# Recurrence of an RWKV layer: products spread over four quadrants of the TensorE array by exchanging partition halves

## The reference, cut to what matters

```python
def wkv7_scan(r, decay, k, v, kk, a):
    def step(S, inp):
        r_t, w_t, k_t, v_t, kk_t, a_t = inp
        s_kk = jnp.einsum('bhij,bhj->bhi', S, kk_t)
        S = (S * w_t[:, :, None, :] - s_kk[..., None] * (a_t * kk_t)[:, :, None, :]
             + v_t[..., None] * k_t[:, :, None, :])
        return S, jnp.einsum('bhij,bhj->bhi', S, r_t)
    ...
y = wkv7_scan(rh, heads(decay), kh, vh, kk, heads(a))
y = layer_norm(y, LNX_EPS).reshape(B, T, RWKV_WIDTH) * lnx_g + lnx_b
```

## Time and profile before

| what | value |
|---|---|
| median of three runs | 3341.51 us |
| profiled execution, its span | 3339.61 us, 3337.8 us |
| PE busy in the span | 3075.4 us (92%) |
| DVE, ACT, POOL busy | 1552.5, 1104.6, 984.9 us |
| PE instructions | 21074 matmuls |
| the recurrence, first to last product but the turned y | 387.8 to 642.6 us |

### The profile page before, as it was taken

The page is one execution under the profiler, slowest core; times in us unless marked ns, Lnnn a source line. Parts: engine busy times, 40 slices in busy tenths (PEclk is TensorE's granted clock), DMA queues, the critical chain, the costliest instruction groups (busy, mean ns, idle before and its releaser), DMA issues. The chain is left out here.

```text
span 3337.8 us, 50028 instructions
## 1 busy us (share of the span) xinstructions
PE 3075.4 (92%) x21074; PEld 2436.7 (73%) x21074; DVE 1552.5 (47%) x2316; ACT 1104.6 (33%) x1885; POOL 984.9 (30%) x638
## 2 busy tenths in 40 slices
PE   5999799795999998998999999789989999996898
PEld 3886489674888887887877777567778777775676
DVE  3999745434332333244034433378431434424875
ACT  3012333233222222123134434455222444445532
POOL 2442022202333333332233333142223333331421
PEclk8999899897999999999999999899999999998999
DMA  5112400032111111122212112576431122127754
GB/s 205 45 51 85 150 4 4 27 114 95 50 45 49 50 45 40 51 98 89 70 46 82 64 62 84 186 221 186 148 105 52 50 71 82 51 76 261 203 160 140
DMA packets 341929, 308.57 MB, mean 92 GB/s; under 512 B 11328, under 2 KB 300480, under 8 KB 337248
## 3 DMA queue, kind: packets, MB, share of 16 engines
q1 hardware_dynamic: 266944, 242.63, 23.0%
q10 hardware_dynamic: 74784, 63.05, 5.7%
HBM read 248.89 MB, written 54.66 MB: 91 GB/s over the span
## 5 line engine op out<-in xcount | busy, mean ns | idle before, releaser
L1871 PE MATMUL PS<-x_high_sb,w_high_sb 128*128 128x512 f32 x1312 | 530.0, 404 | 0.0
L1871 PE MATMUL PS<-x_high_sb,w_low_sb 128*128 128x512 f32 x1312 | 518.2, 395 | 0.0
L1871 PE MATMUL PS<-x_low_sb,w_high_sb 128*128 128x512 f32 x1312 | 517.4, 394 | 0.0
L1871 PEld LDWEIGHTS PS<-x_high_sb,w_high_sb 128*128 128x128 f32 x1312 | 247.0, 188 | 76.0 <-issue 23.9
L1871 PEld LDWEIGHTS PS<-x_high_sb,w_low_sb 128*128 128x128 f32 x1312 | 246.9, 188 | 57.7
L360 PE MATMUL PS<-h_high_sb,up_high_sb 128*128 128x512 f32 x704 | 274.8, 390 | 13.5 <-POOL up_low_sb L1436 13.5
L1871 PEld LDWEIGHTS PS<-x_low_sb,w_high_sb 128*128 128x128 f32 x1312 | 247.3, 189 | 52.3
L1486 DVE SCALAR_TENSOR_TENSOR z_sb<-PS,cols_sb,z_sb 128x1023 f32<-128x1023 f32 x88 | 112.8, 1282 | 348.5 <-ACT z_sb L1467 342.1
L360 PE MATMUL PS<-h_low_sb,up_high_sb 128*128 128x512 f32 x704 | 274.6, 390 | 0.0
L360 PE MATMUL PS<-h_high_sb,up_low_sb 128*128 128x512 f32 x704 | 274.4, 390 | 0.0
L2109 DVE CUSTOM_DVE_ANT_0 scores_sb<-PS,alibi_sb,sinks_sb 128x256 f32<-128x256 f32 (+1 forms) x256 | 104.4, 464 | 342.2 <-PE PS L1889 342.2
(11 more groups left out here) (405 smaller groups left out, 6090.0 us busy)
## 6 DMA issues: line engine op xcount, KB each, us to landing
w_raw_sb<-w_in SPq DMA_DIRECT2D x102, 512.0 KB, 3.7
up_raw_sb<-w_up SPq DMA_DIRECT2D x44, 512.0 KB, 3.7
ada_slots_sb<-ada_w SPq DMA_DIRECT2D x16, 1024.0 KB, 6.7
attn_raw_sb<-attn ACTq DMA_DIRECT2D x32, 512.0 KB, 5.9
decays_sb<-running_sums SPq DMA_DIRECT2D x16, 1024.0 KB, 7.4
attn_raw_sb<-state_out ACTq DMA_DIRECT2D x32, 512.0 KB, 4.0
xbc<-staged_sb ACTq DMA_DIRECT2D x24, 512.0 KB, 2.6
xbc_sb<-xbc SPq DMA_DIRECT2D x16, 768.0 KB, 9.0
```

The source lines that it names most:

```text
L1871: last = pe.matmul(PS[:, bank, :], a[:, n % 2, k], b[:, k, cols], start=k == 0 and a is WH and b is HH, stop=k == KT - 1 and a is WL)
```

## The change

Nine of a unit's steps (AP1, SQ2a, SQ2b, GV, AP2, SQ3, FR, FF, Z) are given all four quadrants. `by_quarter` takes, for each of its three operands, a rule of where a pair (head parity, chunk) lies. In *plain* all lie by chunk, as before. In *first* the odd heads' chunks have changed partition halves; in *home* chunk c is on half c, but the slots are sorted by which half the chunk came from; in *away* the halves are changed with those slots. Each product reads one layout and writes another, and its result lies in two banks (the number in the table goes from 1 to 2), 256 columns in each. `N` writes the odd heads exchanged, `PB` writes its second half for odd heads exchanged (two products in place of one), and at the copy of the fourth token tile ACT writes four half-partition pieces in place of two whole ones.

`AP1` and `AP2` no longer add to the inverse. DVE writes, beside each power, power plus identity into the (then free) transition tile, and the product with that is simply copied. The products of y with the state leave `S0` and are issued together in `S1`. The table's costs are new, and with them the order.

```diff
-        steps = [("PB", 2, "dve", 1.2), ("N", 2, "dve", 0.6), ("TRa", 2, "act", 1.8), ("SQ1a", 1, "dve", 1.0),
+        steps = [("PB", 2, "dve", 1.1), ("N", 2, "dve", 0.6), ("TRa", 2, "act", 1.8), ("SQ1a", 1, "dve", 1.0),
...
+        quarters = [(f, par, c) for f in range(CT) for par in range(2) for c in range(2)]
+        plain = lambda f, par, c: (half(c), CT * par + f)
+        first = lambda f, par, c: (half(c ^ par), CT * par + f)
+        home = lambda f, par, c: (half(c), CT * (c ^ par) + f)
+        away = lambda f, par, c: (half(c ^ par), CT * c + f)
...
+            def by_quarter(bank, left, left_at, right, right_at, out_at, width=CH, stop=True, check=False):
+
+                for f, par, c in quarters:
+                    (rows, i), (_, j), (out, n) = left_at(f, par, c), right_at(f, par, c), out_at(f, par, c)
+                    at = n % CT * width
+                    last = pe.matmul(PS[out, bank + n // CT, at:at + width], left[rows, i], right[rows, j],
+                                     start=width == CH or f == 0, stop=stop, skip_group_check=check)
+                return last
...
+                        if par == 0:
+                            pe.matmul(PS[half(c), b0, f * P:(f + 1) * P].rearrange("p (a n) -> p a n", a=2), left, right,
+                                      start=True, stop=True)
+                        else:
+                            pe.matmul(PS[half(c), b0 + 1, f * P:f * P + CH], left, right[:, 0], start=True, stop=True)
+                            last = pe.matmul(PS[half(1 - c), b0 + 1, f * P + CH:(f + 1) * P], left, right[:, 1],
+                                             start=True, stop=True)
...
-                    last = by_chunk(b0, PW2[:, g, 0], IB[:, g])
+                    last = by_quarter(b0, PI[:, g], first, IB[:, g], first, home)
...
-                    last = by_chunk(b0, PW2[:, g, 1], PW2[:, g, 0])
+                    last = by_quarter(b0, PW2[:, g, 1], first, PW2[:, g, 0], first, home)
...
-                    last = by_chunk(b0, IB[:, g], XR[:, g], P, True, False, True)
+                    last = by_quarter(b0, IB[:, g], away, XR[:, g], away, home, P, False, True)
...
-                    for f in range(CT):
-                        last = pe.matmul(PS[half(c), 4 * g + 2, hcol(2 * f + c)], RKQ[feat(c), f, chunk(c)],
-                                         state(k, c)[feat(c), f], start=False, stop=True, skip_group_check=True)
+                    for f, d in [(f, d) for f in range(CT) for d in range(2)] if c else []:
+                        last = pe.matmul(PS[half(d), 4 * g + 2, hcol(2 * f + d)], RKQ[feat(d), f, chunk(d)],
+                                         state(k, d)[feat(d), f], start=False, stop=True, skip_group_check=True)
...
-                    for par in range(2):
-                        nc.scalar.copy(XR[:, g, 4 * par:4 * par + 4, 0:HD], tok[:, g, 3].rearrange(
+                    for par, c in [(par, c) for par in range(2) for c in range(2)]:
+                        nc.scalar.copy(XR[half(c ^ par), g, CT * c:CT * (c + 1), 0:HD], tok[half(c), g, 3].rearrange(
                             "p (f a c) -> p a f c", f=CT, a=2)[:, par])
...
-                elif name in ("SQ1a", "SQ2a"):
-                    ins = v.tensor_copy(flat((PW2 if name == "SQ1a" else PW4)[:, g, 0]), B)
-                elif name in ("AP1", "AP2", "AP3"):
+                elif name == "SQ1a":
+                    v.tensor_copy(flat(PW2[:, g, 0]), B)
+                    ins = v.tensor_tensor(PI[:, g], by_head(B), ident_rows, ALU.add)
+                elif name == "SQ2a":
+                    v.tensor_copy(slots(PW4[:, g, 0]), two)
+                    ins = v.tensor_tensor(slots(PI[:, g]), two, ident_of, ALU.add)
+                elif name in ("AP1", "AP2"):
+                    ins = v.tensor_copy(slots(IB[:, g]), two)
+                elif name == "AP3":
                     ins = v.tensor_tensor(flat(IB[:, g]), flat(IB[:, g]), B, ALU.add)
```

More of the change, by code:

```diff
@@ L893, in rwkv_recurrence @@
             for i, (name, n, eng, cost) in enumerate(steps):
[L894 to L898, removed]
+                if name == "GT":
+                    own = (3,)
+                elif n in choice:
+                    own = min((o for o in choice[n] if name != "F2" or not set(o) & set(banks_of["Z"])),
+                              key=lambda o: max(used[b] for b in o))
                 else:
@@ L909, in rwkv_recurrence @@
         count, filled, emptied, before, last_in, done = {"act": 0, "dve": 0}, {}, {}, {}, {}, 0
-        for k, g, name, eng, banks in plan:
+        for k, g, name, eng, own in plan:
             key = (k, g, name)
@@ L918, in rwkv_recurrence @@
             joins = name in ("H1", "H2", "S0", "S1", "YX", "Y")
-            before[key] = [] if joins else sorted({last_in[b] for b in banks if b in last_in})
+            before[key] = [] if joins else sorted({last_in[b] for b in own if b in last_in})
             if eng is not None:
-                for b in banks:
+                for b in own:
                     last_in[b] = key
@@ L957, in _ @@
                     empty(pe, other)
-                b0 = banks[0]
+                b0 = own[0]
                 cols = unit_cols(k)
@@ L1002, in _ @@
                     empty(pe, (k, g, "TRa"))
-                    for f, par, i, h in every:
-                        for c in range(2):
-                            last = pe.matmul(PS[half(c), b0, i * CH:(i + 1) * CH], GR[half(c), g, i, 1],
-                                             v[half(c), hcol(h)], start=True, stop=True)
+                    for f, par, c in quarters:
+                        (rows, i), (out, n) = plain(f, par, c), away(f, par, c)
+                        at = n % CT * CH
+                        last = pe.matmul(PS[out, b0 + n // CT, at:at + CH], GR[rows, g, i, 1], v[rows, hcol(2 * f + par)],
+                                         start=True, stop=True)
                 elif name == "AP2":
@@ L1054, in _ @@
                                       v[half(c), hcol(h)], start=f == 0, stop=False, skip_group_check=True)
[L1055 to L1058 removed]
+                    for f, par, c in quarters:
+                        rows, i = home(f, par, c)
+                        pe.matmul(PS[feat(par), b0 + c, f * HD:(f + 1) * HD], nb[rows, hcol(2 * f + par)],
+                                  WU[rows, g, i, HD:P], start=False, stop=False, skip_group_check=True)
                     for f, par, i, h in every:
@@ L1062, in _ @@
                                       start=h == 0, stop=False, skip_group_check=True)
-                    for f, par, i, h in every:
-                        for c in range(2):
-                            last = pe.matmul(PS[half(c), b0 + 2, hcol(h)], BR[half(c), g, i, 0], WU[half(c), g, i, HD:P],
-                                             start=False, stop=False, skip_group_check=True)
+                    for f, par, c in quarters:
+                        (rows, i), (_, j) = home(f, par, c), plain(f, par, c)
+                        last = pe.matmul(PS[rows, b0 + 2, hcol(2 * f + par)], BR[rows, g, j, 0], WU[rows, g, i, HD:P],
+                                         start=False, stop=False, skip_group_check=True)
                 elif name in ("S0", "S1"):
@@ L1157, in _ @@
             root(TT - 1)
-            for k, g, name, eng, banks in plan[-2:]:
-                turned((k, g, name), banks[0])
+            for k, g, name, eng, own in plan[-2:]:
+                turned((k, g, name), own[0])
         @block.gpsimd
@@ L1253, in _ @@
                 elif name == "MT":
[L1254 to L1255 removed]
+                    ins = v.tensor_tensor(MT[:, g], two, ident_of, ALU.add)
                 elif name == "ZT":
```

96 lines of the change are left out of this document (49 added, 47 removed), and 10 rows, old and new, of the table steps.

## The result

| kernel | median us (runs) | range us | profiled execution us | its span us |
|---|---|---|---|---|
| before | 3341.42 (15) | 3334.11 to 3342.55 | 3339.61 | 3337.8 |
| after | 3346.39 (15) | 3342.53 to 3354.36 | 3345.06 | 3343.3 |

The ratio is 1.0021, 95% interval 1.0013 to 1.0029: the change costs 5 us by the medians, 4 to 10 us by the interval. The forecast was 3343.0 us, "the same".

What follows compares the result with a forecast made beforehand. It took PE's queue as the bound. Full periods +5.0, unit 0 +1.3, two periods without norm work -1.7 and the end -3.1 gave +1.5 us on 3341.5: 3343.0 us, own range 3337 to 3350.

Steps and rivals of the forecast that it cites:

- All six waits: PE waiting for DVE or ACT emptyings before H2, SA, SQ2b, PG, SQ3 and FR: 6.25 us a period.
- PE's step: Each changed 64-wide step on PE takes 0.48 us over four quadrants, bounds 0.44 and 0.60, in place of 0.93.
- rivals on four quadrants: Four quadrants don't overlap in the exchanged order, the eight steps stay at 0.93 us: 3367 us, chance 0.03.
- work that arrives in full or in part: PE's saved work shows up in the time: 3304 us in full, chance 0.05; 3332 in part, chance 0.12.
- The rival of later emptyings: Emptyings come later than walked, mainly from AP1 to SQ3: 1.6 us a period more, 3354 us, chance 0.20.
- the walk: Step-by-step comparison along the new order of PE's own work with the emptying engine's queued work, one period: 31.75 us.
- H2: PE waits before H2 for H1's emptying on DVE, with only TRa between: 1.7 us in place of 0.4.
- FR: PE waits before FR for GV's emptying on ACT, four pieces and the main copy: 1.1 us.
- -3.1 us at the end: FF and Z lie inside the last period and one S0 is short by 0.46 us: -3.1 us together.
- a full period: One recurrence period: 30.7 - 0.4 - 4.8 + 6.25 = 31.75 us, 1.0 us longer, five times.
- The rival did not occur: The clock falls in the recurrence because waits make PE idle: some 50 us, 3390 us, chance 0.03.
- The rule weighed in the prediction: Tiling speeds TensorE but not PSUM emptying, so time comes near the forecast sum; busy shares would give near 3304 us.

Runs made afterwards that it cites:

- Run 3: The changed kernel with all layouts plain, so each changed step uses two quadrants again, same order and additions: 3370.67 us, ratio 1.0091.
- run 6: The changed kernel with the fourth token tile's copy (GV's operand) in two whole pieces, its exchange left out: 3342.97 us, ratio 1.0012.
- Run 4: The changed kernel with y_gated moved on DVE from behind F2 to behind H1: 3338.97 us, ratio 0.9998.
- run 2: The kernel before with the changed table's nominal costs, so only the order changes: 3363.69 us, ratio 1.0068.
- run 7: The changed kernel with a cost table chosen so that the walked order has few waits: 3323.79 us, ratio 0.9951.
- run 12: The changed kernel with a third cost table, from a walk that also limits how fast 253 PE instructions pass: 3323.11 us, ratio 0.9957.
- Run 1: The changed kernel with the planner's old costs, bank counts and all else of the change kept: 3325.27 us, ratio 0.9958.
- run 10: Run 1's kernel measured again, unchanged: 3325.86 us, ratio 0.9956.
- run 8: Run 7's kernel with two more 128x512 products a unit on PE, their result overwritten: 3335.09 us, ratio 0.9990.

## Why the prediction came out as it did

The mechanism was right. All six waits are there, behind the engines named, and in the full periods there is nothing else of size. Two of its signs were missed all the same: the period of F2 goes up to 33.2 us, where 31.2 to 32.2 was said, and PE's busy time in the recurrence is 212.5 us, where about 205 was said. Point by point:

- **PE's step.** Predicted 0.48 us, measured 0.41 to 0.52. Run 3 shows that the quadrants work in the exchanged order. The rivals on four quadrants (3367) and on work that arrives in full or in part (3304, 3332) are out. The rival of later emptyings (3354) holds in part: of its 1.6 us a period 0.55 are there.
- **The emptyings on the path.** Predicted 6.25 us a period. Measured 5.8 us of idle time, to which six tails of about 0.17 us belong, since the walk counts from start to start (0.93 us for a step whose record is 1.10): 6.8 us. With the tails H2 is 1.77 against 1.7, SA 1.19 against 1.2, SQ2b 0.52 against 0.4, PG 1.26 against 1.35, SQ3 0.58 against 0.5, FR 1.50 against 1.1. FR is the largest miss: four pieces took 1.65 us and not 1.24, at the upper end of the bounds given. The walk also named ACT alone for it; by run 6 AP3's emptying on DVE holds FR 0.9 us even where the pieces are short.
- **H2 was right by luck.** DVE took 569.42 - 562.44 = 6.98 us from Y's first instruction to the end of H1's emptying, where the walk had 6.7: y_gated took 0.4 us more by GpSimd's addition beside it. The walk's own numbers give 6.7 - 4.9 = 1.8 us, and 2.0 with the release that the other five places have, where it wrote 1.7. PE also took some 0.4 us more up to H2 (PB with F2, and a pause of 0.21). Without the first H2 would wait 1.4 us. Run 4, which moves y_gated out of both, gives back 7.4 us.
- **The sum.** It had -3.1 us at the end (measured: 21.28 us from the last but one Y to the last product before, 17.96 after, -3.3), and for the six periods from Y to Y -0.85 + 5 x 1.0 = +4.2 us, where 184.51 went to 192.85, +8.3 us. Up to the first Y it had 1.3 - 0.85 = +0.4, and it was +0.2. That agreement is in part luck: the stage starts at the lower clock, which lasted 4.8 us of it before and 2.8 us now, and the walk had no term for it. So the miss, 5.2 against 1.5, is the term "a full period": +1.8 us (32.5 against 30.8 us), and not +1.0. Of the missing 0.8 us, 0.55 are the six waits; that the rest are steps at 0.52 us and pauses fits the rows, but no run separates it.
- **The clock.** The rival did not occur in the profiled execution: behind the first 2.8 us of the stage it stayed at 1.00, with PE idle for 6 of 32 us in pieces of 0.4 to 1.8 us. That was nearer than it looks. In runs 2 and 3 the clock fell once each behind a 1.8 us wait before H2, the very wait that after has (up to 1.81 us), while the same wait in their other periods was followed by no fall. Runs 7 and 12 have seven waits of 2.0 to 2.5 us, and at or behind the end of five of them it fell. Each fall cost 1.7 us; the rival's 50 us had the clock low for a third of the stage. The page "TensorE: Matmul & The Clock Gate" of the Trainium skill warns, under "A second HAM failure mode: psum-queue depth-cycling", of short idle times between groups of products. After's trace doesn't show it; in four other traces single waits of 1.8 to 2.5 us were followed by a fall.
- **The rule weighed in the prediction** held for this order. "TensorEngine Tiling (Array Packing)" of the Trainium skill says, under "Performance Considerations", that the emptying of PSUM may become the bottleneck once tiling makes the products quick; by the engines' busy shares the time would have been 3304 us. Run 1, with the same quick products and 21 us less, shows that it was the order that put the emptyings on the path, not their amount.

Where the prediction was off in kind is what it left unasked: whether the order had to be this one. The same change with the old costs is 21 us faster than with the new ones and 15 to 16 us faster than the kernel before (runs 1 and 10). Of the new orders none was told from it.

What stays open: what a faster order would give if the small operation of Y's emptying didn't meet GpSimd's multiplication. By the rows, run 7 lost 8.2 us to the waits behind it and 3.4 to falls of the clock, run 12 up to 7.3 and 5.1. Taken away in full that would put them near 3312 and 3311 us, an estimate from these rows that no run tests; moving that one multiplication on GpSimd is the run that is missing. Why some long waits were followed by no fall (2.05 and 2.18 us in run 7, a pause of 2.2 us in run 8, most of the 1.8 us waits) stays open, and so does the exact rule of the pauses: run 8 had more of them than my reading foretold.

## What to carry to other kernels

When steps on the bounding engine get shorter, price the order of the steps anew before the gain: each step that stood between a product and its emptying was cover, and cover shrinks with it. Change the work and the planner's costs in separate runs, since here one gave 16 us and the other took 22. An operation that stands between two emptyings is a candidate to move by one place first: that edit of one word gave 7 us. And when a new order gives less than the walk says, look in its trace for operations that have grown: here one of 0.17 us had become 2.2 us.

## What the runs showed of the hardware that was not expected

- **DVE beside GpSimd.** The same product of two SBUF operands, 128x512 in f32, takes 0.68 us alone, 0.98 where it overlaps an operation of GpSimd for 0.43 us (its multiplication, before) and 1.38 where for 0.83 us (its addition, after). The page "GPSIMD Engine Reference" of the Trainium skill, section "1. Specifications", says that VectorE and GpSimd share their SBUF interfaces and contend when a VectorE instruction has two SBUF inputs; these rows agree, and DVE's copies and masks that read PSUM beside it kept their 0.68 us. A much smaller operation lost more: the one on 128x8 in Y's emptying, 0.17 us alone, took 2.1 to 2.2 us in four units each of runs 7 and 12 and 0.5 us in four of run 8, and all twelve end about 0.03 us behind the end of GpSimd's 2.36 us multiplication.
- **Pauses at places of PE's instruction stream.** With products 64x64 over four quadrants PE pauses 0.2 to 2.2 us at multiples of about 253 recorded instructions. The page "Runtime: NRT & Kernel Launch" of the Trainium skill, section "Instruction fetch mechanics", tells of blocks of 256 instructions and calls the cost of a crossing mostly hidden. The places agree; with stretches of 3.65 us it is not hidden, and run 10 pays 8.4 us for it. That it is the next block which is late is a reading: the runs show the places alone.
- **Half the partitions aren't half the time on ACT.** A 64x256 copy and a 128x256 one both have records of 0.40 us (after and run 6); the four 64x256 pieces of after start 0.41 us apart, the two 128x256 ones 0.31.
- **The clock can fall behind a single wait.** In run 7 it went to its lower level 1.1 us behind the end of a 2.0 us wait, and stayed there for 3.4 us; in run 2 it did so 0.5 us behind one of 1.8 us. PE had been busy up to each of these waits. Other waits of the same length, in the same runs and in after, were followed by no fall.
